# Sliding-window attention's scores as whole-array products of stacked query parts, with rotations, stacks and copies in new places

## The reference

```python
yA = forgetting_attention(...)           # "fox": softmax with a decay added to the logits
yB = dsa_attention(rope(qB), rope(kB), vB, ...)   # "dsa": one key head for 8 query heads, top 256 keys
r  = retention(rope(qC), rope(kC), vC)   # "ret"
yD = sliding_window_gqa(rope(qD), rope(kD), vD, sinks)   # "swa"
# swa: 8 query heads share 2 key heads; block b of 128 tokens sees blocks b-1 and b
logits = einsum('bnqgrd,bnkgd->bngrqk', qb, kband) * d ** -0.5
m = maximum(max(logits), sink); p = exp(logits - m); p = p / (sum(p) + exp(sink - m))
```

## Time and profile before

| what | value |
| --- | --- |
| median of 3 runs | 3039.32 us (3037.69 to 3039.84) |
| profiled execution | 3039.78 us, of which the span is 3037.8 us |
| PE busy | 2988.0 us, 98% of the span |
| DVE, ACT, POOL busy | 1391.3, 1289.9, 1398.2 us |
| layer 0, scores of the weave | about 1085 to 1246 us (fox, dsa), 1293 to 1373 us (swa) |
| layer 1, the same | 2122 to 2284 us, 2330 to 2410 us |

### The profile page before, as it was taken

How to read it: one execution, slowest core, us unless ns; L and a number is a source line. 1 busy time by engine, 2 the same in 40 slices (tenths; PEclk the granted TensorE clock), 3 DMA queues, 4 the chain that set the end, 5 groups by cost and what they waited for, 6 DMA issues and landing times.

```text
span 3037.8 us, 39928 instructions
## 1 busy us (share of the span) xinstructions
PE 2988.0 (98%) x15302; PEld 2438.1 (80%) x15302; DVE 1391.3 (46%) x2189; ACT 1289.9 (42%) x2219; POOL 1398.2 (46%) x1002
## 2 busy tenths in 40 slices
PE   8999999999999999999999999999999999999998
PEld 7778887788888777878888888878787788878887
DVE  7874351421113878562116433168776520264322
ACT  5443443433333446554234444244564533354432
POOL 5345574444444543234455454554332354544543
PEclk9999999999999999999999999999999999999999
DMA  5234242233333423223333333244231233333332
GB/s 158 83 112 144 87 132 91 77 97 97 99 97 85 142 69 89 53 67 87 97 93 99 94 97 99 83 109 138 68 91 42 64 98 97 97 94 97 97 97 71
DMA packets 214891, 287.61 MB, mean 95 GB/s; under 512 B 42682, under 2 KB 122610, under 8 KB 213042
## 3 DMA queue, kind: packets, MB, share of 16 engines
q1 hardware_dynamic: 212210, 279.88, 31.5%
q0 software_dynamic: 880, 2.99, 0.3%
q10 hardware_dynamic: 1616, 2.23, 0.2%
HBM read 269.80 MB, written 4.72 MB: 90 GB/s over the span
## 4 chain that ended last, share of the span: by engine, by line
PE 89%; DVE 6%; ACT 2%; POOL 1%; issue 1%; DMA 0%; ACTq 0%; SPq 0%; DVEq 0%
PE half L732 80%; PE half L1169 1%; PE half L1155 1%; PE half L1226 1%; POOL wL L2917 1%; PE half L1138 1%; PE half L1133 1%; DVE arena L2082 1%; DVE arena L2681 1%; DVE arena L2715 1%; PE half L987 0%; PE half L1004 0%; DVE rms L2073 0%; PE half L1212 0%; DVE arena L2706 0%
## 5 line engine op out<-in xcount | busy, mean ns | idle before, releaser
L2917 POOL TENSOR_TENSOR wL<-slot,wH 128x512 fp32r<-128x512 f32 (+1 forms) x976 | 1366.5, 1407 | 1610.1 <-ACT wH L1336 1609.0
L1336 ACT ACTIVATE wH<-slot 128x512 fp32r<-128x512 f32 (+1 forms) x976 | 603.4, 625 | 1229.3 <-PE half L732 1223.7
L732 PE MATMUL half<-nH,wH 128*128 128x512 f32 x2336 | 922.6, 395 | 8.1 <-POOL wL L2917 3.1
L732 PE MATMUL half<-nH,wL 128*128 128x512 f32 x2336 | 910.2, 390 | 0.0
L732 PE MATMUL half<-nL,wH 128*128 128x512 f32 x2336 | 909.7, 389 | 0.0
L732 PE MATMUL half<-arena_split,wH 128*128 128x512 f32 (+1 forms) x2432 | 735.8, 385 | 1.7 <-issue 0.8
L732 PEld LDWEIGHTS half<-nH,wH 128*128 128x128 f32 x2336 | 438.5, 188 | 119.7 <-issue 20.2
L732 PEld LDWEIGHTS half<-arena_split,wH 128*128 128x128 f32 x2432 | 451.2, 188 | 94.6 <-issue 3.4
L732 PEld LDWEIGHTS half<-nH,wL 128*128 128x128 f32 x2336 | 438.5, 188 | 92.6
L732 PEld LDWEIGHTS half<-nL,wH 128*128 128x128 f32 x2336 | 438.8, 188 | 89.2 <-issue 1.4
L732 PE MATMUL half<-arena_split,wL 128*128 128x512 f32 (+1 forms) x1216 | 466.4, 384 | 0.0
(11 more groups left out here) (351 smaller groups left out, 2656.5 us busy)
## 6 DMA issues: line engine op xcount, KB each, us to landing
slot<-in_w_in SPq DMA_DIRECT2D x344, 256.0 KB, 2.7
slot<-in_w_up SPq DMA_DIRECT2D x440, 128.0 KB, 2.2
slot<-in_w_down SPq DMA_DIRECT2D x132, 256.0 KB, 2.6
slot<-in_w_branch SPq DMA_DIRECT2D x64, 256.0 KB, 2.6
slot<-in_w_out SPq DMA_DIRECT2D x48, 256.0 KB, 2.8
slot<-in_w_gate SPq DMA_DIRECT2D x88, 128.0 KB, 2.1
arena<-arena SPq DMA_DIRECT2D x40, 256.0 KB, 4.4
slot<-in_w_proj_b SPq DMA_DIRECT2D x16, 256.0 KB, 2.9
```

The lines of the kernel that those rows point to most:

```text
L732: mm = pe.matmul(dst, lhsT, rhs, start=(k == 0 and m == 0), stop=(k == last and m == 2))
L1336: act.activation(wH[:, p, 0:cols], slot[:, s, 0:cols], ACT.Copy).then_inc(weights_high, 1)
L2917: pool.tensor_tensor(wL[:, p, 0:cols], slot[:, s, 0:cols], plainly(wH[:, p, 0:cols]), ALU.subtract)\
```

## The change

Names are as before; lines of the changed file are some 16 to 60 higher.

1. swa's scores become whole-array products. `kDH` (rounded keys, laid over the cos and sin tables in `consts`) and `kDL` (remainders, over `qz`) stand for `kDD`, and each pair of query heads gets a stack. Since the tables are overwritten, SP loads them again for layer 1.
2. The stacks and the pieces of the rotations stand at new iterations: `STACK_A`, `STACK_S` and `pieces`.
3. The retention output's gating on VectorE is moved amid iteration 1 of `WEAVE_S`; the copy of one bank of `bgt2a` is moved ahead; cross attention's last unit of `awq1` signals half way, and ScalarE copies its first half then; two roundings of `bup2` are moved ahead of the convolution of group 1.

```diff
-STACK_AT = (9, 11, 17, 21)
+STACK_A = {5: ("dsa", 0), 9: ("dsa", 1), 18: ("dsa", 2), 22: ("dsa", 3), 28: ("key", "swa"), 29: ("swa", 0)}
+STACK_S = {-2: ("swa", 1), 6: ("swa", 3)}
...
-        kBH, kBL, kII, kDD, selb = R(11056, T), R(11568, T), A(17408, T), qz, A(12080, 1152)
-        stack = [R(18432, 2, T), R(26624, 2, T)]
+        kBH, kBL, kII, kDD, selb = R(11056, T), R(11568, T), A(17408, T), qz[:, :, :], A(12080, 1152)
+        stack = {("dsa", 0): R(18432, 2, T), ("dsa", 1): R(26624, 2, T), ("dsa", 2): R(18432, 2, T), ("dsa", 3): R(26624, 2, T),
+                 ("swa", 0): R(18432, 2, T), ("swa", 1): R(24576, 2, T), ("swa", 2): R(11264, 2, T), ("swa", 3): R(12288, 2, T)}
+        tables = consts[:, 4 * P + T:4 * P + 3 * T]
+        kDH, kDL = consts_split[:, 4 * P + T:4 * P + 3 * T].rearrange("p (a b) -> p a b", b=T), qz_split[:, :, :]
...
+                if l + 1 < LAYERS:
+                    sp.wait_ge(S["heads_scores"], (l + 1) * len(STEPS))
+                    sp.dma_start(tables, I["consts"][:, 4 * P + T:4 * P + 3 * T]).then_inc(S["moved"], 16)
                 gate(3, 0)
...
-                    unit(ps[1], "awq1", k, stream)
+                    if k < KD - 1:
+                        unit(ps[1], "awq1", k, stream)
+                    else:
+                        unit(ps[1], "awq1", k, stream, part=[0, 1]).then_inc(S["bank_done"], 1)
+                        unit(ps[1], "awq1", k, stream, part=[2, 3]).then_inc(weights_used, 1)
...
-                    if br == "dsa":
-                        pe.wait_ge(S["stack_rest"], l * STACKED + 1 + i + 1)
+                    if br != "fox":
+                        pe.wait_ge(S["stack_rest"], stacked((br, i), l))
                         for p in range(2):
-                            for m, keys in enumerate((kBH, kBL)):
-                                mm = pe.matmul(half[:, S_AT[p]:S_AT[p] + n], stack[i % 2][:, p, b * P:b * P + P], keys[:, 0:n],
+                            for m, keys in enumerate((kBH, kBL) if br == "dsa" else (kDH[:, i // 2], kDL[:, i // 2])):
+                                mm = pe.matmul(half[:, S_AT[p]:S_AT[p] + n], stack[br, i][:, p, b * P:b * P + P], keys[:, k0:k0 + n],
...
+                    if ("bgt2a", KD - 1) in weave.at(it):
+                        done(act, "bgt2a", l)
+                        act.wait_ge(S["yc_split"], l + 1)
+                        evac_by_bank(gate_b[2], jobs.half["bgt2a"], part=[0])
...
-                def stack_high(i):
+                def stack_high(br, i):
 
-                    if i == 0:
+                    if br == "key":
+                        act.wait_ge(S["roped"], PRIMED + l * 5 + 5)
+                        act.activation(kDH, kDD, ACT.Copy).then_inc(S["stack_high"], 1)
+                        return
+                    if (br, i) == ("dsa", 0):
                         act.wait_ge(S["roped"], PRIMED + l * 5 + 2)
...
+                    elif (br, i) == ("swa", 2):
+                        act.wait_ge(S["yc_split"], l + 1)
...
                 for it in WEAVE_S.its:
+                    if it == 4:
+                        stack_high("swa", 2)
                     woven(WEAVE_S, it, then, gate_read)
+                    if it in STACK_S:
+                        stack_high(*STACK_S[it])
...
-                    if 0 < g < NG - 1:
+                    if g == 1:
+                        round_units("bup2", l, 0, [6, 7], 512)
+                    elif 0 < g < NG - 1:
                         others(f"bup{g + 1}", l)
...
+                    if g == 0:
+                        round_units("bup2", l, 0, [4], 512)
                     act.wait_ge(S["ff_ready"], l * NG + g + 1)
                     round_ff(conv[:, p, 0:2, :], g)
+                    if g == 0:
+                        round_units("bup2", l, 0, [5], 512)
...
-                pieces = {0: ("bqB", qB, 1, [0]), 1: ("bqB", qB, 1, [1]), 3: ("bqB", qB, 1, [2]),
-                          7: ("bqC", qC, 2, [1]), 9: ("bqC", qC, 2, [2]),
-                          13: ("bkC", kC, 3, [0]), 15: ("bkC", kC, 3, [1]), 17: ("bkC", kC, 3, [2]),
+                pieces = {-1: ("bqB", qB, 1, [0]), 0: ("bqB", qB, 1, [1]), 1: ("bqB", qB, 1, [2]),
+                          4: ("bqC", qC, 2, [0]), 8: ("bqC", qC, 2, [1]), 12: ("bqC", qC, 2, [2]),
+                          14: ("bkC", kC, 3, [0]), 16: ("bkC", kC, 3, [1]), 18: ("bkC", kC, 3, [2]),
                           26: ("bqD", qD, 4, [0]), 27: ("bqD", qD, 4, [1]), 28: ("bqD", qD, 4, [2])}
...
-                    woven(WEAVE_A, it, ("bqC", qC, 2, [0]) if it == 6 else None)
+                    woven(WEAVE_A, it)
                     if it in pieces:
                         rope(*pieces[it])
...
                 for it in WEAVE_S.its:
-                    woven(WEAVE_S, it)
+                    woven(WEAVE_S, it, retained_gated if it == TURN_C else None)
+                    if it - 1 in STACK_S:
+                        rest_of(*STACK_S[it - 1])
+                    elif it == 4:
+                        rest_of("swa", 2)
```

More of the change, by code:

```diff
@@ L349, in two_blocks @@
         rms = sb("rms", T)
[L350 removed]
+        with nc.sbuf_tensor("qz", [P, 2, T], F32) as qz:
+            pass
+        qz_split = ctx.enter_context(nc.sbuf_tensor("qz_split", [P, 2, T], F32R))
         small = sb("small", 168)
@@ L476, in two_blocks, with stacked @@
         SEL_AT = (None, 0, 256, 640)
-        STACKED = 1 + PAIRS
+        STACKS = [("key", "dsa")] + [("dsa", i) for i in range(PAIRS)] + [("key", "swa")] + [("swa", i) for i in range(PAIRS)]
+        def stacked(what, l):
+            return l * len(STACKS) + STACKS.index(what) + 1
         forward = [[(0, 512, 0, 0)], [(1, 384, 512, 512), (3, 128, 896, 896)], [(2, 256, 1024, 1024)]]
@@ L1108, in _ @@
                 half = ps[1]
-                queries = {"fox": Q, "swa": qD}
+                queries = {"fox": Q}
                 nth = l * len(STEPS)
@@ L1113, in keys_at @@
                     rows = slice(HD * p, HD * p + HD)
-                    return K[rows, i, k0:k0 + n] if br == "fox" else kDD[rows, i // 2, k0:k0 + n]
+                    return K[rows, i, k0:k0 + n]
                 def values_at(br, i, p, j):
@@ L1344, in others, with evac_by_bank @@
                 round_units(name, l, i, range(SPLITS, ring.units[name]), cols)
-            def evac_by_bank(to, h, func=ACT.Copy, **kw):
-                for j in range(4):
+            def evac_by_bank(to, h, func=ACT.Copy, part=range(4), **kw):
+                for j in part:
                     ins = act.activation(to[:, j, :], ps[h][:, j * T:j * T + T], func, **kw)
@@ L1889, in mixer_read @@
                     if name == "bqC":
-                        act.wait_ge(S["stack_rest"], l * STACKED + 1)
+                        act.wait_ge(S["stack_rest"], stacked(("key", "dsa"), l))
                         evac_by_bank(qC, h)
@@ L1909, in decays @@
                     ins.then_inc(S["ret_decay"], 1)
-                def stack_high(i):
-                    if i == 0:
+                def stack_high(br, i):
[4 more added lines that the diff above has]
+                    if (br, i) == ("dsa", 0):
                         act.wait_ge(S["roped"], PRIMED + l * 5 + 2)
-                    if i >= 2:
+                    elif br == "dsa" and i >= 2:
                         act.wait_ge(S["heads_scores"], nth + 4 * PAIRS + 4 * (i - 1))
+                    elif (br, i) == ("swa", 0):
+                        act.wait_ge(S["heads_scores"], nth + 4 * PAIRS + 4 * 3)
+                    elif (br, i) == ("swa", 1):
+                        act.wait_ge(S["ret_scores_read"], l * 12 + 12)
+                    elif (br, i) == ("swa", 2):
+                        act.wait_ge(S["yc_split"], l + 1)
+                    whole = qB if br == "dsa" else qD
                     for p in range(2):
                         rows = slice(HD * p, HD * p + HD)
-                        ins = act.activation(stack[i % 2][rows, p, :], qB[rows, i, :], ACT.Copy)
+                        ins = act.activation(stack[br, i][rows, p, :], whole[rows, i, :], ACT.Copy)
                     ins.then_inc(S["stack_high"], 1)
@@ L2651, in _, with rest_of @@
                 first, second = slice(0, HD), slice(HD, P)
-                stack_rest(0, (kBL[first, :], kBL[second, :]), [mix1[first, 2, :]] * 2, [kBH[first, :]] * 2)
+                stack_rest(stacked(("key", "dsa"), l), (kBL[first, :], kBL[second, :]), [mix1[first, 2, :]] * 2, [kBH[first, :]] * 2)
+                def rest_of(br, i):
+                    if br == "key":
+                        stack_rest(stacked((br, i), l), (kDL,), (kDD,), (kDH,))
+                        return
+                    of, whole = stack[br, i], qB if br == "dsa" else qD
+                    stack_rest(stacked((br, i), l), (of[second, 0, :], of[first, 1, :]), (whole[first, i, :], whole[second, i, :]),
+                               (of[first, 0, :], of[second, 1, :]))
```

(2 more changed lines are left out.)

65 lines of the change are left out of this document (33 added, 32 removed).

## The result

The changed kernel takes **3056.14 us** (median of 6 runs, 3053.36 to 3059.11), the kernel before 3038.51 us in the same session (median of 6, 3037.11 to 3045.9). The ratio is 1.0058, with a 95% interval of 1.0047 to 1.0069: 17.6 us slower, where 3051 was forecast. The profiled execution of the changed kernel took 3059.11 us, its span is 3057.3 us.

The account below looks back on a forecast made before the run. TensorE, 98% busy, was taken as the bound. Gains 6.0 + 5.3 = 11.3 against losses 16.0 + 5.8 + 1.4 = 23.2 gave 11.9 us slower: 3051 us, 8 in 10 within 3032 to 3060.

Parts of the forecast that it names:

- What bounds the kernel, and where the change acts: TensorE, busy 98%, so only its work and waits count; most of the change acts on VectorE inside the weave.
- Scores, 6.0 us gained: swa's whole-array score steps get shorter on TensorE: 3.0 us a layer, 6.0 us gained, bounds 4.5 to 7.5.
- Waits removed, 5.3 us: TensorE's waits on gating (1.6), `bup2` remainders (2.6) and the `awq1` copy (1.1) go: 5.3 us gained, 4 to 6.
- Even iterations, 16.0 us lost: Rotations and stacks between late normalising and next maxima make TensorE wait at scores: 8.0 us a layer, 16.0 us lost.
- the upper bound: Even iterations' loss if GpSimd's remainders lengthen pieces to 3.38 us and bias may be held too: 11 us a layer.
- Keys, 5.8 us lost: Keys' rounding on ScalarE at iteration 28 waits for the last rotation, delaying step 30's turn: 5.8 us lost, 4 to 8.
- Third stack, 1.4 us: At iteration 4 ScalarE waits for swa's third stack's remainder ahead of two weight roundings: 1.4 us lost, 0 to 2.
- Clean ports: Rotations never meet GpSimd, normalising ends 1 us earlier: 10.0 us lost there, keys 5.0, time 3040 to 3045; chance 0.2.
- VectorE as a backlog: VectorE's lateness is one queue, so less work before step 14 brings 7.9 us faster, 3031; chance 0.22.
- Concurrent halves: Products on separate row halves already run concurrently, so swa's new scores gain nothing: 3057; chance 0.05.

Follow-up runs that it names:

- experiment 1: Changed kernel with only its rotations and dsa stacks put back at the iterations of the kernel before: 3035.56 us.
- experiment 2: Kernel before with only the new places of the rotations and dsa stacks: 3060.91 us.
- experiment 3: Kernel before with only the new sliding scores, their stacks, keys' rounding and table reload; old places, no small edits: 3040.53 us.
- experiment 4: Kernel before with only the four small edits (gating, `bgt2a` bank, `awq1` copy, `bup2` roundings): 3033.31 us.
- experiment 6: Changed kernel with ScalarE's weight rounding at iterations 5 and 9 moved behind that iteration's exponentials: 3055.7 us.
- experiment 12: Changed kernel with even-iteration pieces and stack remainders between maxima and normalising, keys at 29, first swa stack at 31, third's high part behind 4: 3029.73 us.
- experiment 7: Changed kernel with ScalarE's weight roundings at iterations 5, 6, 9 and 10 moved behind the exponentials: 3054.33 us.
- experiment 5: Changed kernel with rotation pieces of iterations 4, 8, 12, 14, 16, 18 moved between the maxima and the normalising: 3044.78 us.

## Why the prediction came out as it did

**What bounds the kernel, and where the change acts:** right. Nearly all of the loss is in TensorE's waits in the first weave and in the low clock behind them, and experiments 1 and 2 put it on the places of the rotations and stacks.

**Scores, 6.0 us gained:** right. Without its waits, swa's stretch from the first to the last scores is 3.3 us shorter in experiment 3 (layer 0), and in the changed kernel it is 76.5 - 1.5 = 75.0 us beside 79.8 - 1.4 = 78.4 before: 3.33 us a layer, 6.7 in all.

**Waits removed, 5.3 us:** right; 4.3 us by experiment 4. In the list of waits the remainders stand at 4.9 - 2.6 + 1.4 = 3.7 us, just the sum's terms.

**Even iterations, 16.0 us lost:** the mechanism was right and the sum close, 19.6 - 6.2 = 13.4 us at fox's scores and 5.2 - 1.2 = 4.0 at dsa's, 17.4 in all. That closeness is in part luck, for the places differ. For a layer: 4 and 8 cost 2.8 us each where I had 2.0; 6 cost 1.5 where I had 0.8; 12 cost the 0.7 that I had; 14 and 16 cost 0.55 and 0.78 and 18 nothing, 1.3 where I had 2.4; and the wait at step 15, behind iteration 10, fell by 0.35, where I let it stay. The waits came at steps 17, 19 and 21 and not at 19, 21 and 23. At 4 and 8 the term that was too small is the duration of the bias, 2.38 us instead of 1.40: it met a second remainder. I had kept that for the upper bound ("bias after it may be held as well"). The piece's own 1.1 us more was mostly paid for by the normalising, which no longer met that remainder (0.75 us for its two halves, 1.76 in the earlier trace rows). The Trainium skill (SBUF — State Buffer, section Who interferes with whom) has this as an exclusive lock; the trace agrees, and experiment 6 shows it by moving the remainder: the piece fell from 3.36 to 2.29 us.

**What no term held: the clock.** This is the step that failed: the sum gave the stretch behind a wait nothing, and in the profiled execution the clock was low behind three waits of the weave (the scores of step 9 in both layers, the turn of step 30 in layer 0), 5.1 us in all by the windows. At 980 us, ahead of the two layers of the second block, the low clock cost 3.4 us instead of the 1.7 of before; at 50 us and at 2020 us it cost 1.7 us in both. The rest of the account is what I had forecast: the waits are 18.2 us more (16.0 + 5.8 + 1.4 - 5.3 = 17.9 in my terms) and the scores give 6.7 back, 11.5 us beside my 11.9. With the clock it is 11.5 + 5.1 + 1.7 = 18.3 of the 19.5 us between the spans; 1.2 us I can't place. This holds for the profiled execution, the slowest of the six (mean clock 0.995). The others had 0.996 to 0.998, and even the two at 0.998 took 3053.4 and 3054.0 us. How the 17.6 us between the medians divide, their times don't tell.

**Keys, 5.8 us lost:** right in cause, 7.2 - 1.9 = 5.3 us by the waits. The rounding began when the last piece was done, as written.

**Third stack, 1.4 us:** 0.70 us a layer at the weight behind it, as written.

**The rivals.** Clean ports: the normalising did end earlier, as it said, but pieces and bias met remainders all the same. VectorE as a backlog: step 7 waited 1.2 us as before, step 15 1.5 instead of 1.9, and the pieces at 4 and 8 caused 2.8 us each; it falls. Concurrent halves: falls by the starts.

Left open: experiment 2 lost 23.3 us, experiment 3 lost 2.9 and experiment 4 gained 4.3; the sum is 21.9 and the change itself 17.6. The intervals are wide enough for it, and I can't say whether parts of the change help each other. Which of two equal waits the clock falls behind is open as well, and so is why iterations 14 and 18 had room in experiment 12 where 12 and 16 had not.

## What to carry to other kernels

An engine at 46% busy can still set the time: look for where its late input and its next deadline lie closest, and put movable work where the gap is long. Here that was worth 20 us for the iterations and 6.5 us for the place within the even ones; the arithmetic saved 6.7 us. Don't price a stall of the bounding engine by its length alone; look at the granted clock behind it. And where two engines are released by the same third one, moving one instruction away from a collision tends to move the collision.

## What the runs showed of the hardware

TensorE's granted clock fell to 1.2 GHz behind 13 of 20 waits of 2.7 to 2.8 us, not the same ones in each execution, and was 0.66 to 0.67 as a mean over the next 5 us in most of them and 0.50 in two; behind waits of 0.8 to 1.9 us it did so 4 times in some 100. A mean of 0.66 put the next scores off by 1.6 us, one of 0.50 by 2.3 us (13.67 us between the starts instead of 11.38, experiment 2). VectorE's instructions that met a weight's remainder on GpSimd took 1.0 to 1.1 us longer: two-input ones (2.28 to 3.36 us), and TENSOR_SCALAR with one array as input, too (1.52 us instead of 0.49 for the second of two of 512 columns in experiment 7). A stack's remainder went from 1.39 to 3.37 us for its two halves. It goes the other way, too: a weight's remainder that began while a piece ran took 2.35 us (experiment 5). Four fast matmuls of 256 columns on the whole array made a step of 0.48 us, while two fp32 ones on separate halves of the rows took 0.84 us.
